# One head further ahead in the gated recurrence: the next head's first direction moved half a head sooner

## The chip, the core and the metric

The kernel runs on one core of one Trainium2 chip. The metric is the device time of one execution in microseconds (us). The engines are TensorE (PE), VectorE (DVE), ScalarE (ACT), GpSimd (POOL) and SyncE (SP, which here issues the DMAs); each works through its own queue in order, and they meet at semaphores.

## The reference, cut to what matters

One layer of a hybrid model: adaLN-modulated RMSNorm, one input projection shared by four retention heads and four heads of a gated linear recurrence (HGRN2), an output projection, then a top-4-of-32 expert FFN. The change touches the recurrence alone. Per head and per direction (forward, backward) over 256 context and 1024 latent tokens:

```
f = lb + (1 - lb) * sigmoid(z)          # z = u @ w_z, per direction
k = 1 - f;  log_a = log(f);  q = silu(u @ w_q);  v = u @ w_v
b = cumsum(log_a) within a chunk
state' = exp(b_end) * state + (k * exp(b_end - b))^T v
out    = causal(q * decay * k) v + (q * exp(b)) state
```

The outputs of both directions are summed, normalised per head and multiplied with a swish gate.

## The kernel before

The stage is `hgrn2`. It holds the projected channels of a head on 128 partitions and the 1280 tokens in the free dimension, in ten tiles of 128 tokens (two context, eight latent). Products of fp32 accuracy are three passes (high, low parts), so one projection of 512 tokens is 24 matmuls. The four heads run one after the other. Head h has two halves: tiles 0 to 3 and tiles 4 to 7.

**PE, for each head h.** Per half `scores` of four tiles and `output` of four, interleaved. Between them stand the projections of the next head: `gates_of_keys(h+1, i)` for i = 0 to 5 (direction d = i // 3; 256, 512 and 512 tokens) and `queries(h+1, 0 and 1)`. After the last `output` come six `turn_keys(h+1, n)` (transposes of the decayed keys), `updates(h+1)` (20 products of turned keys and values) and `gates_of_keys(h+2, 0)` and `(h+2, 1)`. The turned keys go alternately to two PSUM banks, `h_tb` and `h_po`; each has to be copied out by ACT (`turned_keys`) before the bank is written again.

**ACT.** It copies projections out (`copy_z`), splits weights (`high_chunk`), does `logs` (sigmoid of both directions, then log of both), `key_decays` (exp for both directions), `query_sig`, `query_decays`, `totals`, the copies of turned keys, the exps of seven `levels` per half (the first of them as 16 small activations in `first_level`), `roots` (squares of the outputs) and `gate_sig`.

**DVE.** `pick` masks the scores of a tile, `cumulate` scans the logs, `keys`, `decayed_keys` and `decayed_queries` multiply, `level` multiplies the exps of a level with keys and queries, `states` runs the nine-step state chain of a direction, `finish` scales four output tiles, `low_chunk` makes the low parts of the weights.

**POOL.** The subtractions of levels 1 to 6 of each half (four per level), the inverse roots, the gates.

**What sets the order.** Every engine's order is written out by hand, in the loops printed below; there is no planner. The waits that matter for the change:

- `turned_products` waits for the low weights of its chunk (`cw_low`) and, through `group_read`, until the bank used two projections before is read. For `gates_of_keys(h+2, 0)` that reader is DVE's `queries(h+1, 0)`.
- `scores(h, 0)` waits for `states` of direction 0, and for level 6 of that half (`lev_ready`). `scores(h, 3)` and `output(h, 0)` wait for the states of both directions; `output(h, 0)` also for both decayed queries.
- the bank `h_po` holds a half's outputs. `turn_keys` that writes it waits until `finish` has read them.
- `high_early` (ACT, last head only) waits for all `updates`; `low_early` on DVE and `early_rows` on PE, which is work of the next stage done early, wait for it in turn.

Of the kernel before, what the change touches and what calls it, by code (L numbers as in the profile page):

```python
# [366 lines left out]
def hgrn2(nc, m, dram, keep):  # L367
# [3 lines left out]
    with ExitStack() as ctx:  # L371
# [104 lines left out]

        def group(h, i):

            return i if h == 0 else LT + GROUPS * h + i
# [134 lines left out]
        def _(pe):  # L614
# [32 lines left out]
            def gates_of_keys(h, i):  # L647
                d, j = divmod(i, 3)
# [42 lines left out]
            def turn_keys(h, n):  # L691
# [4 lines left out]
                if n == 1:  # L696
                    pe.wait_ge(S["o_ready"], LT * h)
                pe.wait_ge(S["ktok_ready"], 6 * h + max(0, n - 1))
                for i in range(min(4, NT - 4 * g)):
                    c = 4 * g + i  # L700
                    tt = pe.transpose(tb[n % 2][:, i * P:(i + 1) * P], kdec[d][:, c * P:(c + 1) * P], ident[:])
                tt.then_inc(S["turned"], 1)

            def updates(h):
# [4 lines left out]
                for n in range(6):  # L709
                    d, g = divmod(n, 3)  # L710
                    pe.wait_ge(S["ktok_ready"], 6 * h + n + 1)
# [65 lines left out]
            updates(0)  # L777
            for x in range(LT + 2, 2 * LT):
                output_gates(x)
            gates_of_keys(1, 0)  # L780
            gates_of_keys(1, 1)
            for h in range(HEADS):
# [5 lines left out]
                if more:  # L788
                    gates_of_keys(h + 1, 2)
                else:  # L790
# [18 lines left out]
                if more:  # L809
                    for n in range(6):  # L810
# [10 lines left out]
        def _(act):  # L821
# [35 lines left out]
            def copy_z(h, i):  # L857
                d, j = divmod(i, 3)
# [9 lines left out]
            def logs(h):  # L868
                for d in range(2):
                    act.wait_ge(S["z_copied"], 6 * h + 3 * d + 3)  # L870
                    for x, _ in key_pieces(h, d):
                        act.activation(x, x, ACT.Sigmoid).then_inc(S["z_sig"], 1)
# [4 lines left out]
                for d in range(2):  # L877
                    act.wait_ge(S["z_sig"], 4 * h + 2 * d + 2)
                    for (x, _), (to, _), (ahead, _) in zip(key_pieces(h, d), cum_pieces(h), ahead_pieces(h)):
                        act.activation(ahead[:, :, 1:STEP] if d else to, tiles(x) if d else x, ACT.Ln, scale=bound[:, h, d, 1:2], bias=bound[:, h, d, 0:1]).then_inc(S["logf"], 1)  # L880

            def key_decays(h):
                act.wait_ge(S["cumulated"], 6 * h + 3)
# [5 lines left out]
                act.wait_ge(S["cumulated"], 6 * h + 6)  # L889
                act.wait_ge(S["gate_part"], h)  # L890
                for x, part in ahead_pieces(h):
                    act.activation(tiles(kdec[1][:, part]), x[:, :, 0:P], ACT.Exp).then_inc(S["exped"], 1)
# [11 lines left out]
            def totals(h):  # L904
                for x, part in cum_pieces(h):
                    act.activation(total[:, 0, part.start // P:part.stop // P], tiles(x)[:, :, P - 1], ACT.Exp).then_inc(S["totals"], 1)
                for x, part in ahead_pieces(h):
# [10 lines left out]
            def turned_keys(h, n):  # L918
# [4 lines left out]
                act.activation(ktok[d][:, 4 * g:4 * g + m_, :], tb[n % 2][:, 0:m_ * P].rearrange("p (i n) -> p i n", i=m_), ACT.Copy).then_inc(S["ktok_ready"], 1)  # L923
# [79 lines left out]
            logs(0)  # L1003
            value(4)
            value(5)
            key_decays(0)
# [3 lines left out]
            totals(0)  # L1010
# [12 lines left out]
            for x in range(6, 2 * LT):  # L1023
# [3 lines left out]
                if x == LT + 2:  # L1027
                    high_chunk(3)
            gate_sig(0)
# [1826 lines left out]
```

## Time and profile before

| | us |
|---|---|
| three runs | 2736.5, 2736.6, 2742.73 (median 2736.6) |
| profiled execution, span | 2736.2 |
| first scores of head 0, 1, 2, 3 | 209.9, 290.7, 371.6, 464.6 |

The profile was taken on one execution of 2736.2 us, 0.4 us under the median. The recurrence's four heads fill some 300 us of it, from 210 to 507. Times below are counted from the start of the span. "Busy" of PE counts the modelled ends of pipelined matmuls; the starts are exact.

### The profile page before, as it was taken

How to read it: one execution, taken by the hardware profiler on the slowest of the kernel's cores; microseconds unless marked ns; L12 is line 12 of the kernel's file. 1: busy time of each engine (PE TensorE's matmuls, PEld its weight loads, DVE VectorE, ACT ScalarE, POOL GpSimd, SP SyncE). 2: the span in 40 equal slices, each digit the busy share in tenths (PEclk: the TensorE clock that was granted, in tenths of full speed). 3: DMA queues.
4: the chain of work that ended last, by engine and by line, in shares of the span. 5: the costliest groups of instructions: out<-in, count | busy, mean ns of one | idle time of the engine just before them, and what ended most of it. 6: DMA issues, size and time to landing. Idle time of an engine off the chain costs nothing.

```text
span 2736.2 us, 46067 instructions
## 1 busy us (share of the span) xinstructions
PE 2587.9 (95%) x16405; PEld 2212.7 (81%) x16406; DVE 2045.3 (75%) x2500; ACT 1453.7 (53%) x1639; POOL 539.6 (20%) x423
## 2 busy tenths in 40 slices
PE   7998987999896999999999999999999999999995
PEld 3896866777885888777887979899989897898885
DVE  5447888545765987999879787866686778978786
ACT  5446565214443765777557465544454546645554
POOL 0035565200023112121212111110121112111111
PEclk9999998999998999999999999999999999999998
DMA  7121011442333996999879697866586779968783
GB/s 289 39 88 44 22 42 57 173 152 93 109 92 127 386 364 229 365 360 359 287 260 362 235 313 258 283 208 209 190 301 206 247 249 314 344 209 296 261 309 133
DMA packets 274722, 606.26 MB, mean 222 GB/s; under 512 B 21788, under 2 KB 52932, under 8 KB 273520
## 3 DMA queue, kind: packets, MB, share of 16 engines
q1 hardware_dynamic: 254256, 561.62, 57.1%
q0 software_dynamic: 20384, 43.51, 6.9%
q8 instruction: 55, 0.90, 0.1%
q14 instruction: 27, 0.22, 0.0%
HBM read 582.09 MB, written 46.97 MB: 230 GB/s over the span
## 4 chain that ended last, share of the span: by engine, by line
PE 40%; issue 10%; DVE 8%; ACT 4%; DMA 4%; DVEq 1%; POOL 1%; ACTq 0%; POOLq 0%
PE e_acc L2488 7%; PE e_acc L2491 7%; PE e_acc L2489 7%; PE e_acc L2461 5%; PE e_acc L2463 5%; PE e_acc L2462 5%; DMA list_now<-lists 3%; DVE e_slot_r L2646 3%; ACT whi L2574 3%; PE e_tb L2430 1%; DVE yo L2733 1%; DVE e_glu L2709 1%; PE e_acc L2523 1%; DVE e_xlo L2655 1%; POOL sum L2388 1%
## 5 line engine op out<-in xcount | busy, mean ns | idle before, releaser
L2574 ACT ACTIVATE whi<-e_slot 128x2048 fp32r<-128x2048 f32 x296 | 561.0, 1913 | 393.7 <-PE e_acc L2491 327.0
L2646 DVE TENSOR_TENSOR e_slot_r<-e_slot,whi 128x2048 fp32r<-128x2048 f32 x296 | 674.6, 2286 | 106.3 <-ACT whi L2574 106.3
L2488 PE MATMUL e_acc<-e_xhi,whi 128*128 128x256 f32 x1664 | 398.8, 282 | 3.3 <-ACT e_xhi L2578 3.3
L2574 ACT ACTIVATE whi<-slot 128x2048 fp32r<-128x2048 f32 x148 | 283.2, 1913 | 192.4 <-PE e_acc L2463 192.4
L2646 DVE TENSOR_TENSOR slot_r<-slot,whi 128x2048 fp32r<-128x2048 f32 x151 | 344.7, 2285 | 18.1 <-ACT whi L2574 16.5
L2461 PE MATMUL e_acc<-whi,e_ahi 128*128 128x512 f32 x800 | 319.4, 399 | 0.0
L2488 PEld LDWEIGHTS e_acc<-e_xhi,whi 128*128 128x128 f32 x1664 | 313.1, 188 | 6.3 <-ACT e_xhi L2578 6.3
L2463 PE MATMUL e_acc<-whi,e_alo 128*128 128x512 f32 x800 | 313.4, 392 | 0.0
L2462 PE MATMUL e_acc<-e_slot_r,e_ahi 128*128 128x512 f32 x800 | 311.5, 389 | 0.0
L2388 POOL DMA_INDIRECT sum<-yo,e_idx_now x48 | 117.8, 2454 | 973.3 <-issue 518.9
L2461 PE MATMUL e_acc<-whi,e_xhi 128*128 128x512 f32 x768 | 303.6, 395 | 1.8 <-DVE e_slot_r L2646 1.6
L2463 PE MATMUL e_acc<-whi,e_xlo 128*128 128x512 f32 x768 | 302.0, 393 | 0.0
L2334 POOL DMA_INDIRECT e_xg<-v_rows,e_idx_next x74 | 152.3, 2058 | 499.4 <-issue 346.5
L2491 PE MATMUL e_acc<-e_xlo,whi 128*128 128x256 f32 x1664 | 212.7, 282 | 0.0
L2491 PEld LDWEIGHTS e_acc<-e_xlo,whi 128*128 128x128 f32 x1664 | 204.3, 188 | 0.0
L2489 PE MATMUL e_acc<-e_xhi,e_slot_r 128*128 128x256 f32 x832 | 199.2, 281 | 0.0
L2489 PE MATMUL e_acc<-e_xhi,slot_r 128*128 128x256 f32 x832 | 198.0, 280 | 0.0
L2463 PEld LDWEIGHTS e_acc<-whi,e_alo 128*128 128x128 f32 x800 | 149.7, 187 | 34.9
L2462 PEld LDWEIGHTS e_acc<-e_slot_r,e_ahi 128*128 128x128 f32 x800 | 150.4, 188 | 30.9
L2461 PEld LDWEIGHTS e_acc<-whi,e_ahi 128*128 128x128 f32 x800 | 150.5, 188 | 28.6
L2461 PEld LDWEIGHTS e_acc<-whi,e_xhi 128*128 128x128 f32 x768 | 144.6, 188 | 35.3 <-DVE e_slot_r L2646 5.7
L2463 PEld LDWEIGHTS e_acc<-whi,e_xlo 128*128 128x128 f32 x768 | 144.0, 188 | 33.8
(432 smaller groups left out, 5014.9 us busy)
## 6 DMA issues: line engine op xcount, KB each, us to landing
e_slot<-in_w SPq DMA_DIRECT2D x296, 1024.0 KB, 7.1
slot<-in_w SPq DMA_DIRECT2D x151, 1024.0 KB, 6.4
rv<-in_w_ada SPq DMA_DIRECT2D x32, 512.0 KB, 5.6
slot<-in_w_in SPq DMA_DIRECT2D x9, 1024.0 KB, 9.6
wa<-in_w_ada SPq DMA_DIRECT2D x8, 1024.0 KB, 17.1
slot<-in_w_in SPq DMA_DIRECT2D x12, 512.0 KB, 4.2
xt<-in_x SPq DMA_DIRECT2D x8, 512.0 KB, 14.7
slot<-in_w_out SPq DMA_DIRECT2D x4, 1024.0 KB, 13.9
```

What stands on the lines that cost most here:

```text
L2334: g.indirect_dma_start(xg[b][:], None, dram["v_rows"], bass.IndirectOffsetOnAxis(ap=idx_next[:, b:b + 1], axis=0), bounds_check=SEQ - 1, o ...
L2388: g.indirect_dma_start(dram["sum"], bass.IndirectOffsetOnAxis(ap=idx_now[:, b:b + 1], axis=0), yo[:, b, :], None, compute_op=ALU.add).then ...
L2430: tt = pe.transpose(tb[bank][:, k * P:(k + 1) * P], src[:, (4 * at + k) * P:(4 * at + k + 1) * P], ident[:])
L2461: pe.matmul(out, hi[:, k, c], wh, start=False, stop=False)
L2462: pe.matmul(out, hi[:, k, c], wl, start=False, stop=False)
L2463: return pe.matmul(out, lo[:, k, c], wh, start=False, stop=last)
L2488: pe.matmul(out[:, c, :], whi[i % RING][:, w], xhi[:, kk, :], start=first, stop=False, skip_group_check=True)
L2489: mm = pe.matmul(out[:, c, :], wlo[i][:, w], xhi[:, kk, :], start=False, stop=False, skip_group_check=True)
L2491: mm = pe.matmul(out[:, c, :], whi[i % RING][:, w], xlo[:, kk, :], start=False, stop=(kk == KT - 1), skip_group_check=True)
L2523: pe.matmul(out[:, b, :], pick2[:], bias[:, j * 512:(j + 1) * 512], start=True, stop=False)
L2574: act.activation(whi[i % RING][:], raw[i % PIECES][:], ACT.Copy).then_inc(S["whi_made"], 1)
L2646: v.tensor_tensor(wlo[i % PIECES][:], raw[i % PIECES][:], whi[i % RING][:].bitcast(F32), ALU.subtract).then_inc(S["wlo_made"], 1)
```

## The change

Nothing is computed otherwise; instructions move in four queues, and some waits change with them.

- **PE.** All three projections of direction 0 of head h+1 stand before head h begins, the one of 512 tokens of the second half first (`columns`). `turn_keys(h+1, 0..2)` stand in the middle of head h, around `queries(h+1, 0)` and the first score of the second half. Behind the last output comes `gates_of_keys(h+2, 0)`, then turns 3 and 4, updates 0 to 2, turn 5, updates 3 to 5, and two more projections. The turned keys use `h_po` for n = 4 only, all others `h_tb`; so each of turns 1, 2, 3 waits for the copy of the one before. This holds for head 0 too.
- **ACT.** Sigmoid, log and decays are done for direction 0 at the start of head h, for direction 1 behind the levels of its second half. The copy of turn n stands between the levels. `first_level(h+1, 0)` stands before `roots(h, 1)`, `query_decays(h+1)` between level 3 and level 4.
- **DVE.** `cumulate`, `keys`, `decayed_keys` of direction 0 stand between and ahead of the levels of head h's second half. `queries(h+1, 1)` and `finish(h, 1)` stand behind level 1 of the next head, both `decayed_queries` behind level 6, ahead of the second `states`.

```diff
+        def columns(h, i):
+            d, j = divmod(i, 3)
+            return d, (2, 0, 1)[j] if h and d == 0 else j
+        def turn_bank(n):
+            return tb[n == 4]
...
-                if n == 1:
+                if n == 4:
                     pe.wait_ge(S["o_ready"], LT * h)
-                pe.wait_ge(S["ktok_ready"], 6 * h + max(0, n - 1))
+                pe.wait_ge(S["ktok_ready"], 6 * h + (0, 1, 2, 3, 3, 4)[n])
...
-            gates_of_keys(1, 0)
-            gates_of_keys(1, 1)
+            for i in range(3):
+                gates_of_keys(1, i)
...
-                if more:
-                    gates_of_keys(h + 1, 2)
-                else:
+                if not more:
                     early_rows(EARLY_FIRST)
...
                     for i in range(3, 6):
                         gates_of_keys(h + 1, i)
+                    turn_keys(h + 1, 0)
                     queries(h + 1, 0)
+                    turn_keys(h + 1, 1)
...
                     scores(h, j)
+                    if more and j == HT:
+                        turn_keys(h + 1, 2)
...
-                    for n in range(6):
-                        turn_keys(h + 1, n)
-                    updates(h + 1)
                     if h + 2 < HEADS:
                         gates_of_keys(h + 2, 0)
+                    turn_keys(h + 1, 3)
+                    turn_keys(h + 1, 4)
+                    updates(h + 1, range(3))
+                    turn_keys(h + 1, 5)
+                    updates(h + 1, range(3, 6))
+                    if h + 2 < HEADS:
                         gates_of_keys(h + 2, 1)
+                        gates_of_keys(h + 2, 2)
...
@@ scalar @@
-                    for i in range(2):
+                    for i in range(1, 3):
                         copy_z(h + 1, i)
+                    key_sigmoids(h + 1, 0)
+                    key_logs(h + 1, 0)
...
                     levels(h, 1, (l,))
+                    if more and l == 0:
+                        key_decays(h + 1, 0)
+                    if more and l == 1:
+                        copy_z(h + 1, 3)
+                        high_chunk(3 * h + 5)
...
+                    if more and l >= 5:
+                        turned_keys(h + 1, l - 5)
...
+                    key_sigmoids(h + 1, 1)
+                    turned_keys(h + 1, 2)
+                    key_logs(h + 1, 1)
+                    if h + 2 < HEADS:
+                        high_chunk(3 * h + 6)
                     query_sig(h + 1, 0)
+                    key_decays(h + 1, 1)
+                    first_level(h + 1, 0)
...
                     query_sig(h + 1, 1)
+                    turned_keys(h + 1, 3)
+                    levels(h + 1, 0, (1,))
+                    turned_keys(h + 1, 4)
+                    levels(h + 1, 0, (2,))
+                    turned_keys(h + 1, 5)
+                    totals(h + 1, 1)
...
+                    levels(h + 1, 0, (3,))
+                    query_decays(h + 1)
+                    levels(h + 1, 0, range(4, NL))
...
@@ vector @@
                     pick(h, 3)
+                    if more:
+                        cumulate(h + 1, 0)
                     for l in range(NL):
                         level(h, 1, l)
+                        if more and l == 0:
+                            keys(h + 1, 0)
+                        if more and l == 1:
+                            decayed_keys(h + 1, 0)
+                        if l == 2 and more:
+                            low_chunk(3 * h + 5)
...
+                if more and now:
                     keys(h + 1, 1)
                     decayed_keys(h + 1, 1)
+                    if h + 2 < HEADS:
+                        low_chunk(3 * h + 6)
+                    queries(h + 1, 0)
                     for l in range(NL):
                         level(h + 1, 0, l)
+                        if l == 1:
+                            finish(h, 1)
+                            queries(h + 1, 1)
...
+                        if l == NL - 2:
                             states(h + 1, 0)
+                    decayed_queries(h + 1, 0)
+                    decayed_queries(h + 1, 1)
                     states(h + 1, 1)
```

## Rows read from the trace of the kernel before

**Rows 1.** Stretches cut at first scores of halves: span, busy PE, PEld, DVE, ACT, POOL, PEclk, DMA.
```profile
209.88:245.95 36.07, 35.00 (x394) 28.54 (x392) 21.73 (x40) 19.77 (x48) 19.08 (x26) 1.00 0.11 31
245.95:290.74 44.79, 34.76 (x406) 29.07 (x404) 42.81 (x79) 32.51 (x81) 29.33 (x28) 0.85 0.19 51
290.74:326.87 36.13, 34.92 (x393) 28.53 (x393) 24.42 (x49) 20.02 (x49) 19.03 (x26) 1.00 0.11 30
326.87:371.57 44.70, 33.62 (x405) 27.91 (x404) 42.75 (x78) 32.49 (x81) 29.26 (x28) 0.89 0.18 52
371.57:407.72 36.15, 34.95 (x392) 28.53 (x393) 24.38 (x49) 20.01 (x49) 19.04 (x26) 1.00 0.06 16
407.72:464.64 56.92, 39.34 (x406) 32.17 (x405) 48.47 (x87) 34.71 (x81) 30.29 (x28) 0.82 0.21 68
```
**Rows 2.** Timeline of PE, turns of head 2's keys: start, duration, count, idle before with releaser.
```profile
347.80 1.09 PE L701 MATMUL h_po<-ident,h_kdec 128*128 128x128 f32 x4 [4.39 <-issue]
...
354.46 1.09 PE L701 MATMUL h_tb<-ident,h_kdec 128*128 128x128 f32 x4 [3.00 <-ACT h_ktok L923]
```
**Rows 3.** Timeline, head 0's setup: third turn on PE, copy of the second on ACT.
```profile
158.35 0.38 PE L701 MATMUL h_tb<-ident,h_kdec 128*128 128x128 f32 x2
...
160.16 0.59 ACT L923 ACTIVATE h_ktok<-h_po 128x512 f32<-128x512 f32 x1
```
**Rows 4.** Timeline of PE at the end of a projection (24 such matmuls) and the next scores.
```profile
326.64 0.39 PE L644 MATMUL h_pj<-uT_r,slot_r 128*128 128x512 f32 x1
326.87 0.38 PE L728 MATMUL h_ps<-slot,h_wk 128*128 128x128 f32 x2
```
**Rows 5.** Timeline of DVE, levels of head 2's first half, first multiplication of several levels.
```profile
356.55 0.83 DVE L1210 TENSOR_TENSOR h_wk<-h_wk,h_keyA 128x256 f32<-128x256 f32 x1
...
359.08 0.83 DVE L1210 TENSOR_TENSOR h_wk<-h_wk,h_keyA 128x256 f32<-128x256 f32 x1
...
362.87 0.41 DVE L1210 TENSOR_TENSOR h_wk<-h_wk,h_keyA 128x256 f32<-128x256 f32 x1
...
365.42 0.28 DVE L1224 COPY h_state<-h_ps 128x128 f32<-128x128 f32 x1
...
368.80 1.69 DVE L1210 TENSOR_TENSOR h_wk<-h_wk,h_keyA 128x256 f32<-128x256 f32 x1
```
**Rows 6.** Timeline of DVE ahead of those levels: keys, second direction, finish, weights, decayed queries, level 0.
```profile
338.18 0.86 DVE L1174 TENSOR_SCALAR h_keyA<-h_keyA,h_bound 128x768 f32<-128x768 f32 x1
...
342.63 0.98 DVE L1174 TENSOR_SCALAR h_keyA<-h_keyA,h_bound 128x768 f32<-128x768 f32 x1
...
346.59 1.12 DVE L1248 SCALAR_TENSOR_TENSOR slot<-h_po,h_ms,slot 128x128 f32<-128x128 f32 x4
...
348.22 1.60 DVE L1143 TENSOR_TENSOR slot_r<-slot,slot_r 128x1024 fp32r<-128x1024 f32 x1
349.74 3.19 DVE L1197 TENSOR_TENSOR slot<-slot 128x1024 f32<-128x1024 f32 x2
352.85 1.14 DVE L1207 TENSOR_TENSOR h_wk<-h_keyA,h_keyA 128x512 f32<-128x512 f32 x1
```
**Rows 7.** Groups of DVE from 326.87 to 371.57: the largest scan, count, busy, mean ns.
```profile
L1158 DVE TENSOR_TENSOR_SCAN h_cumB<-h_scan,h_cumB 128x512 f32<-128x512 f32 x1 | 1.2, 1202 | 0.0
```
**Rows 8.** Timeline of ACT: the three table loads, then the decayed queries' exps to the totals.
```profile
322.30 1.28 ACT L872 ACT_TABLE_LOAD   x1
...
326.24 1.28 ACT L880 ACT_TABLE_LOAD   x1
...
330.91 1.28 ACT L887 ACT_TABLE_LOAD   x1
...
345.39 0.63 ACT L897 ACTIVATE slot<-h_cumA 128x512 f32<-128x512 f32 x1
...
348.77 0.20 ACT L906 ACTIVATE h_total<-h_cumA 128x6 f32<-128x6 f32 x1
```
**Rows 9.** Timeline of PE ahead of head 3: the first early row, after the last update.
```profile
451.33 0.77 PE L686 MATMUL h_pj<-h_early,uhi 128*128 128x512 f32 x1 [9.34 <-DVE slot_r L1151]
```

More of the change, by code:

```diff
@@ L866, in copy_z, with key_sigmoids, key_logs @@
                 act.activation(to, pj[i % 2][:, 0:z - a], ACT.Copy).then_inc(S["z_copied"], 1)
[L868 to L872, printed above, removed]
+            def key_sigmoids(h, d):
+                act.wait_ge(S["z_copied"], 6 * h + 3 * d + 3)
+                for x, _ in key_pieces(h, d):
+                    act.activation(x, x, ACT.Sigmoid).then_inc(S["z_sig"], 1)
+            def key_logs(h, d):
                 if h:
@@ L876, in logs, with key_decays @@
                     gates_out(act, 2 * LT)
[L877 to L883, printed above, removed]
+                act.wait_ge(S["z_sig"], 4 * h + 2 * d + 2)
+                for (x, _), (to, _), (ahead, _) in zip(key_pieces(h, d), cum_pieces(h), ahead_pieces(h)):
+                    act.activation(ahead[:, :, 1:STEP] if d else to, tiles(x) if d else x, ACT.Ln, scale=bound[:, h, d, 1:2], bias=bound[:, h, d, 0:1]).then_inc(S["logf"], 1)
+            def key_decays(h, d):
+                act.wait_ge(S["cumulated"], 6 * h + 3 * d + 3)
+                if d:
+                    act.wait_ge(S["gate_part"], h)
+                    for x, part in ahead_pieces(h):
+                        act.activation(tiles(kdec[1][:, part]), x[:, :, 0:P], ACT.Exp).then_inc(S["exped"], 1)
+                    return
                 act.wait_ge(S["u_done"], 6 * h)
@@ L888, in key_decays @@
                 k.then_inc(S["exped"], 1)
[L889 to L892, printed above, removed]
             def query_decays(h):
@@ L1009, in _ @@
             value(7)
-            totals(0)
+            for d in range(2):
+                totals(0, d)
             value(8)
@@ L1280, in _ @@
                     pick(h, 3)
+                    if more:
+                        cumulate(h + 1, 0)
                     for l in range(NL):
                         level(h, 1, l)
+                        if more and l == 0:
[4 more added lines that the diff above has]
+                            low_chunk(3 * h + 5)
                         if l == 4:
                             finish(h, 0)
-                        if l == 5 and more:
-                            low_chunk(3 * h + 5)
                     pick(h, HT)
-                if more:
-                    cumulate(h + 1, 0)
+                    pick(h, HT + 1)
+                elif more:
+                    cumulate(0, 0)
+                    keys(0, 0)
                 if h == 0:
@@ L1292, in _ @@
                     set_ahead(aheadB[1])
-                if now:
-                    pick(h, HT + 1)
-                    pick(h, HT + 2)
                 if more:
@@ L1322, in _ @@
                             low_early(1)
-                        if now and l == NL - 2:
+                        if l == NL - 2:
                             states(h + 1, 0)
-                    if not now:
-                        low_chunk(3)
-                        states(0, 0)
+                    decayed_queries(h + 1, 0)
+                    decayed_queries(h + 1, 1)
                     states(h + 1, 1)
+                elif more:
+                    decayed_keys(0, 0)
+                    keys(0, 1)
+                    decayed_keys(0, 1)
+                    low_gates(1)
+                    low_gates(0)
+                    queries(0, 0)
+                    queries(0, 1)
+                    decayed_queries(0, 0)
+                    decayed_queries(0, 1)
+                    for l in range(NL):
+                        level(0, 0, l)
+                    low_chunk(3)
+                    states(0, 0)
+                    states(0, 1)
                 else:
```

75 lines of the change are left out of this document (31 added, 44 removed).

## The prediction

> **What bounds the kernel now.** I read the timelines of the four engines over the recurrence, and cut them at the first scores of each half head. In the first halves, PE is busy 35.0 of 36.1 us while DVE is busy for 22 to 24: PE is the bound. In the second halves DVE is busy 42.8 of 44.7 us and PE only 33.6, part of that at 1.2 GHz (granted clock 0.89 and 0.85 of 2.4 GHz) [rows 1]. So the period of 80.8 us is one half bound by PE and one by DVE. What the change is after is PE's idle time in the DVE half: 4.4 us before the second turn and 3.0 us before the fifth, where it waits for ACT, which stands between them in its own queue [rows 2]. All pauses of such a half add up to 44.7 - 33.6 = 11.1 us, and to 56.9 - 39.3 = 17.6 us before head 3 [rows 1].
>
> I count by two marks per head: T, the first scores of the head, and s, the first scores of its second half. Before, T to s is 36.1 us and s to the next T 44.8, 44.7 and 56.9 us [rows 1]. The change puts one projection of 512 tokens, `gates_of_keys(h+1)`, from behind T to ahead of T. It is 24 matmuls of 0.23 to 0.24 us, 5.7 us [rows 4]. To compare alike I take 5.7 off the first halves (30.4 us) and add it to the two middle second halves (50.5 us); the last, s to T of head 3, has no such projection and stays 56.9.
>
> **Part 1: head 0's setup.** Turns 1, 2 and 3 now share one bank, so turn 2 needs the copy of turn 1. PE reached turn 2 at 158.35, and ACT ended that copy at 160.75, because `first_level` stands before it [rows 3]. PE has no pause around there (busy in each slice from 151 to 202), so it moves back by 2.4 us. Cost: **+2.4**.
>
> **Part 2: the first half, T to s.** PE's own work is 30.4 us less its pauses, plus two turns (0.7 us). But DVE now also has the first direction to do here. Its queue from the fourth pick, which ends at T + 9.1, to level 6: three scans, seven levels, keys, decayed keys, the low weights of one chunk, and `finish`.
> - scans 2.9 us when alone (1.2 us for 512 tokens, 1280 tokens in all [rows 7])
> - level 0 in 3.3 to 3.7, levels 1 and 2 in 2.5 each while POOL works, levels 3 to 6 in 1.3 each without it [rows 5, 6]
> - keys and decayed keys 4.5, weights 1.6, finish 1.1 [rows 6]
>
> The sum is 2.9 + 3.3 + 5.0 + 5.2 + 4.5 + 1.6 + 1.1 = 23.6; with seams 23.9: s = T + 33.0. The queries' projection on PE waits for the same queue: its low weights come behind level 2, at T + 26.7, after PE is ready at T + 25.1; then 5.7 us and a turn give T + 32.8. Both paths end together.
>
 So s = T + 34.2 against 30.4 for head 0: **+3.8**.
>
> For heads 1 and 2 the decayed queries are new between level 6 and the second states: 3.2 us [rows 6]. The first scores start at level 6, but `scores(h, 3)` and `output(h, 0)` need both, so DVE brings first 3.2, then 3.4 us of states (365.42 to 368.80 in [rows 5]), then a pick. The first output starts at T + 7.3 instead of T + 4.2: 3.1 more, and everything behind it. **+6.9** for each.
>
> **Part 3: the middle second halves, s to T.** The gain is meant to come here: DVE has 7.4 us less to do. But its queue is now tied to ACT and PE in turn. The chain, from s on:
> - ACT: copy of turn 1, then sigmoid and log of direction 1. A load is 1.28; both directions with the load take 3.9 and 4.7 us, so one takes 2.6 and 3.0 [rows 8]. With a second copy between: s + 6.7.
> - DVE: scans 3.2 (ten of 128 tokens), two picks 2.0, keys and decayed keys 4.5, low weights 1.6, queries 0.7 [rows 6]: s + 18.8.
> - PE: `gates_of_keys(h+2, 0)` waits for the last two of these. It was ready at s + 15.8. The projection 5.7, turn 3: s + 25.0. This is the new head-of-line wait: ACT stands at the copy of turn 3, with the exps of level 1 behind it, and DVE has nothing from s + 22.5 on.
> - ACT: copy and first exp, s + 26.0. DVE: level 1 and `finish`, s + 29.8. Only then may turn 4 write `h_po`.
> - Turn 4, copy, ten updates, turn 5, copy: s + 33.0. ACT: total, one copy, level 3, then `query_decays`, 3.4 us [rows 8], first exp of level 4: s + 38.8.
> - DVE: levels 4 and 5 2.5, states 3.4, level 6 2.5 because the first multiplication meets POOL's gate (1.69 us) [rows 5]: T = s + 47.2.
>
> PE is ready at s + 43.8, so it waits 3.4 us. Against 50.5 that is **-3.3** for each of two heads. The granted clock is taken as 2.4 GHz here, as pauses are shorter than before; what if not is a rival.
>
> Two table loads more lie on this chain in ACT (sigmoid and log are now loaded twice per head), at 1.28 us each; the row after each load starts 0.01 us behind it. The Trainium skill (ScalarE: Activation LUTs, What ACT_TABLE_LOAD costs) gives a switch 1283 ns and a drain of 1380 ns behind it. By that rule each would cost 2.66 us, and the estimate for three heads would be some 8 us higher; the trace shows no drain, and the sum stands without it.
>
> **Part 4: the last second half.** PE has no projection to do, so turn 3 is at s + 16.9 and level 1 follows at s + 24.0, `finish` s + 25.1, turn 4. By then PE has been idle 8 us; I count updates at 1.2 GHz, as the clock fell in the same place before. Updates end at s + 34.9. Before, PE's last update ended at 442.0 (451.33 less 9.34, [rows 9]), s + 34.3: nothing gained. Then `high_early` 3.7, level 3, and now `query_decays` 3.4 us before level 4, behind which `low_early` stands. So `early_rows(0)` starts at s + 47.4 where it was 451.33 - 407.72 = 43.6: **+3.8**. DVE's levels, states and decayed queries end under the 13 us of early rows.
>
> **Sum.** 2.4 + 3.8 - 3.3 + 6.9 - 3.3 + 6.9 + 3.8 = +17.2 us. Behind head 3's first scores nothing is changed, and the next stage starts at a barrier, so the shift stays. On the span of 2736.2 that is 2753.4; the median lies 0.4 above the profiled span: **2754 us**, 0.6% slower. DMAs are no part: the same loads are issued, and those moved (weights of two chunks, the gates behind `finish`) have over 5 us to spare.
>
> **Rivals.**
> - *It does what it is for, faster.* If ACT and PE never hold up each other, DVE alone bounds a period, with 24.4 + 42.8 + 1.2 = 68.4 us [rows 1] against 80.8. Two periods give up to -24.8; allowing half of it, for picks and gates that have to wait anyway, -12.4, with +2.4 of the setup and no loss elsewhere: -10, 2727 us. For it: DVE's work moved away is real. Against: turn 3 behind a projection, and turn 4 behind `finish`. It decides at whether DVE stands idle after level 0. Chance 0.09.
> - *No difference.* Scans pay nothing to POOL (-3.6), and PE reaches T later than DVE, so that the wait of output 0 is hidden (-6.2): 17.2 - 9.8 = +7.4, 2744 us. Chance 0.17.
> - *Slower still, by the clock.* If TensorE's clock falls to 1.2 GHz in the pause before turn 4, as it did in the pause of 4.4 us before [rows 1, 2], ten updates and a turn take twice 2.4 us, and the chain hangs on them: +2.5 for each of two heads, 2759 us. Chance 0.20.
> - The forecast, 2749 to 2757: chance 0.52. The last 0.02 is beyond.
>
> **Range and chances.** 2740 to 2764 leaves out the faster case and the tails. A difference of under 0.3% (8.2 us) is about what a measurement of this kernel can't tell from none. Faster 0.09; same 0.17; slower 0.74.
>
> **What the profile after would show.** First output of heads 1 and 2 over 7 us behind the first scores, instead of 4.2. DVE idle 3 to 4 us in front of level 1 of each next head, released by ACT. PE idle about 3 us before a projection with DVE as releaser, 4 to 5 us before turn 4. Six table loads per head instead of three. First scores of heads 1, 2, 3 near 299, 384 and 482. The prediction is wrong if PE's pause before T is gone, if level 1 on DVE follows level 0 at once, or if the setup costs nothing.

## The result, and the profile after

| | before | after |
|---|---|---|
| median of four runs | 2738.2 us | 2772.8 us |
| profiled execution, span | 2736.2 | 2775.1 |
| first scores of head 0, 1, 2, 3 | 209.9, 290.7, 371.6, 464.6 | 218.1, 308.9, 401.3, 498.5 |
| start of the next stage | 511.8 | 549.8 |

The ratio is 1.0128, with an interval of 1.0113 to 1.0143: 1.3% slower. In the profiles nearly the whole loss stands at the end of the recurrence: 38.0 us of 38.9. Foretold were 17, and the median of 2772.8 us lies outside the stated range of 2740 to 2764. The profile of after was taken on the slowest of its four executions (2776.8, 2776.5, 2769.2 and 2768.9 us), so the steps below may add up to some 4 us more than the median shows.

The stretches of after, cut at the first scores of halves like [rows 1], which they answer (span, busy PE, PEld, DVE, ACT, POOL, granted clock, DMA share, GB/s; the last is head 3's first half):
```profile
218.09:254.17 36.08, 33.03 (x377) 26.91 (x376) 30.62 (x49) 25.34 (x61) 23.85 (x26) 0.91 0.11 30
254.17:308.91 54.74, 40.91 (x423) 34.38 (x421) 32.37 (x68) 31.44 (x70) 22.37 (x28) 0.85 0.18 51
308.91:346.69 37.78, 33.37 (x377) 27.10 (x378) 35.53 (x60) 25.57 (x62) 23.79 (x26) 0.90 0.06 15
346.69:401.33 54.64, 40.54 (x423) 34.06 (x421) 32.53 (x67) 31.45 (x70) 22.37 (x28) 0.85 0.18 52
401.33:440.03 38.70, 34.64 (x376) 27.87 (x377) 34.92 (x60) 25.48 (x62) 23.17 (x26) 0.87 0.01 1
440.03:498.45 58.42, 37.33 (x396) 31.12 (x397) 38.62 (x68) 33.19 (x69) 23.97 (x28) 0.80 0.21 66
498.45:534.91 36.46, 34.71 (x369) 27.79 (x368) 25.01 (x49) 13.96 (x40) 19.72 (x26) 0.91 0.01 2
```
DVE's work did move as meant: the middle second halves have 32.4 us of it instead of 42.8. But they are not shorter, they are 10 us longer, and no engine is busy in them for more than 41 of 54.7 us. The clock is below 1 in every stretch, while before the first halves ran at 1.00.

PE's timeline from the end of head 0's first half to the first output of head 1 (start, duration, line, operation, count, idle before with its releaser):
```profile
245.38 0.77 PE L651 MATMUL h_pj<-uhi,slot_r 128*128 128x512 f32 x1 [2.96 <-DVE slot_r L1185]
...
272.61 0.79 PE L651 MATMUL h_pj<-uhi,slot_r 128*128 128x512 f32 x1 [2.96 <-DVE slot L1221]
...
281.01 0.60 PE L710 MATMUL h_tb<-ident,h_kdec 128*128 128x128 f32 x4
286.48 1.09 PE L710 MATMUL h_po<-ident,h_kdec 128*128 128x128 f32 x4 [4.88 <-issue]
...
308.91 0.76 PE L737 MATMUL h_ps<-slot,h_wk 128*128 128x128 f32 x2 [6.00 <-DVE h_wq L1257]
315.47 0.46 PE L759 MATMUL h_po<-h_val,h_st 128*128 128x128 f32 x2 [1.40 <-DVE h_near L1286]
```
All the foretold waits are there: 2.96 us before the queries' projection and before `gates_of_keys(2, 0)`, 4.88 before turn 4, and 6.00 before T, where 3.4 were counted. The second projection takes from 272.61 to turn 3 at 281.01, 8.4 us, where 5.7 were counted. Most of it ran at 1.2 GHz: its products start 0.43 us apart until 278.7 and 0.23 us apart after that. That was not in the sum. The first output of head 1 starts at T + 6.56, not over 7 us behind T: the two decayed queries took 2.35 us here, 3.19 in [rows 6].

DVE and POOL: level 1 of head 1, and its level 6 with POOL's gates beside it.
```profile
282.79 0.79 DVE L1252 TENSOR_TENSOR h_wk<-h_wk,h_keyA 128x256 f32<-128x256 f32 x1 [8.36 <-ACT h_wk L990]
...
304.29 1.39 DVE L1252 TENSOR_TENSOR h_wk<-h_wk,h_keyA 128x256 f32<-128x256 f32 x1
305.60 2.56 DVE L1253 TENSOR_TENSOR h_wk<-h_wk,h_keyA 128x256 f32<-128x256 f32 x1
```
```profile
303.05 2.35 POOL L1135 TENSOR_TENSOR slot<-h_kdec,slot 128x1024 f32<-128x1024 f32 x1 [17.23 <-ACT h_kdec L950]
305.48 2.40 POOL L1137 TENSOR_TENSOR slot<-slot,h_nw 128x1024 f32<-128x1024 f32 x1
```
DVE stands idle for 8.36 us between level 0 and level 1, waiting for an exp of ACT, which stands behind the copy of turn 3. Some 2.2 us of that are there because level 0 ended sooner than foretold (s + 20.3, not s + 22.5), the rest is the chain. The second multiplication of level 6 begins 0.12 us behind a POOL product and ends 0.3 us behind that product's end. The Trainium skill (SBUF — State Buffer, Who interferes with whom) calls the port that both need an exclusive lock, so that the later one waits out the other's whole instruction. By that rule, the trace agrees here: 2.56 us for 0.41 us of work.

### The profile page after: what moved, and what is told of

It is laid out like the page before. It is cut to its first block, busy times and chain, and to the rows that moved or that the text cites. A ratio compares the mean times of both kernels' runs of the same rounds, so it can differ in the third digit from the quotient of the medians.

```text
span 2775.1 us, 46091 instructions
## 1 busy us (share of the span) xinstructions
PE 2603.0 (94%) x16405; PEld 2225.2 (80%) x16406; DVE 2048.8 (74%) x2500; ACT 1468.4 (53%) x1648; POOL 535.1 (19%) x423
## 4 chain that ended last, share of the span: by engine, by line
PE 39%; issue 10%; DVE 8%; ACT 4%; DMA 4%; DVEq 1%; POOL 1%; ACTq 0%; POOLq 0%
PE e_acc L2543 7%; PE e_acc L2546 7%; PE e_acc L2544 7%; PE e_acc L2516 5%; PE e_acc L2518 5%; PE e_acc L2517 5%; DMA list_now<-lists 3%; DVE e_slot_r L2701 3%; ACT whi L2629 3%; PE e_tb L2485 1%; DVE yo L2788 1%; DVE e_glu L2764 1%; PE e_acc L2578 1%; DVE e_xlo L2710 1%; POOL sum L2443 1%
## 5 line engine op out<-in xcount | busy, mean ns | idle before, releaser
L2518 PEld LDWEIGHTS e_acc<-whi,e_alo 128*128 128x128 f32 x800 | 149.7, 187 | 34.9
L2516 PEld LDWEIGHTS e_acc<-whi,e_xhi 128*128 128x128 f32 x768 | 144.5, 188 | 35.5 <-DVE e_slot_r L2701 5.8
## 6 DMA issues: line engine op xcount, KB each, us to landing
xt<-in_x SPq DMA_DIRECT2D x8, 512.0 KB, 14.9
```

The source lines that it names most:

```text
L2516: pe.matmul(out, hi[:, k, c], wh, start=False, stop=False)
L2518: return pe.matmul(out, lo[:, k, c], wh, start=False, stop=last)
```

## Experiments

Marks as in the prediction: T is the first scores of a head, s those of its second half. "Idle products" are `pe.matmul(ps[2][:, 384:512], ident, ident)`, before the early rows with `pj[0]` in place of `ps[2]`, into columns that nobody reads at that time; they only keep PE busy. The table has all kernels. A ratio is of medians, against runs of the kernel before on the same chip. Marks and spans are of one profiled execution each, and the executions of one kernel lie up to 9.5 us apart (e9: 2736.3 to 2745.9), so a difference of 1 or 2 us between two rows is not shown to be one.

| kernel | T0 | s to T (1, 2, 3) | T to s (0, 1, 2, 3) | stage ends | span | ratio |
|---|---|---|---|---|---|---|
| before | 209.9 | 44.8, 44.7, 56.9 | 36.1, 36.1, 36.2, 32.2 | 511.8 | 2736.2 | |
| after | 218.1 | 54.7, 54.6, 58.4 | 36.1, 37.8, 38.7, 36.5 | 549.8 | 2775.1 | 1.0128 |
| e1_warm | 218.1 | 55.4, 55.4, 64.5 | 35.5, 39.9, 41.1, 31.7 | 556.3 | 2781.7 | 1.0176 |
| e1b_warm_half | 218.0 | 49.9, 49.1, 54.8 | 34.3, 39.1, 39.0, 37.4 | 536.5 | 2769.3 | 1.0109 |
| e2_queries_early | 217.9 | 50.0, 51.1, 59.8 | 34.7, 37.3, 37.6, 32.2 | 535.6 | 2758.5 | 1.0090 |
| e3_turn_first | 218.6 | 44.3, 43.4, 59.3 | 34.9, 38.6, 40.6, 34.8 | 529.4 | 2750.8 | 1.0067 |
| e4_setup_banks | 215.3 | 54.7, 53.3, 58.5 | 36.1, 39.1, 38.7, 36.5 | 547.0 | 2768.3 | 1.0117 |
| e5_turn_queries | 215.3 | 46.4, 48.1, 58.2 | 34.2, 39.8, 35.6, 32.4 | 524.9 | 2747.3 | 1.0049 |
| e6_and_low_queries | 216.1 | 47.9, 46.9, 57.0 | 34.2, 38.0, 36.8, 32.2 | 524.2 | 2747.1 | 1.0036 |
| e7_low_first | 215.3 | 47.3, 49.0, 57.8 | 34.3, 34.8, 36.9, 32.6 | 523.0 | 2747.0 | 1.0039 |
| e8_gates_wait | 218.7 | 48.2, 50.3, 58.9 | 34.9, 41.3, 41.3, 32.3 | 540.8 | 2764.2 | 1.0098 |
| e9_all | 215.6 | 43.1, 43.3, 50.9 | 34.3, 35.7, 34.9, 31.7 | 504.3 | 2740.2 | 1.0016 |
| e10_before_warm | 209.9 | 44.8, 44.7, 52.3 | 35.9, 38.2, 38.1, 31.7 | 510.5 | 2738.9 | 1.0005 |
| e11_all_cold | 215.6 | 46.1, 44.5, 53.2 | 34.3, 34.8, 35.4, 32.5 | 511.4 | 2737.1 | 1.0006 |
| e12_before_late | 210.2 | 44.8, 44.8, 51.8 | 36.2, 36.1, 36.1, 32.9 | 507.8 | 2728.9 | 0.9982 |

### Is it the clock? Idle products in the pauses

e1_warm puts them before the two projections, before turn 4 and before the early rows; e1b_warm_half has the same with 12, 12, 18 (30 in the last transition) and 44.
```
+                    warm(24)
                     queries(h + 1, 0)
...
+                        warm(24)
                         gates_of_keys(h + 2, 0)
                     turn_keys(h + 1, 3)
+                    warm(40 if h + 2 < HEADS else 60)
                     turn_keys(h + 1, 4)
...
+                        pe.wait_ge(S["q_ready"], 2 * HEADS - 1)
+                        warm(80, pj[0])
```

> The changed kernel with idle products of the identity put ahead of PE's waits: 24 before the queries' projection, 24 before the next head's projection, 40 (60 before head 3) before turn 4, 80 before the early rows; a product takes about 0.12 us, so they fill the pauses of 3.0, 3.0, 4.9 and 7.6 us and little more. Theory (the missing loss is TensorE's clock: projections at 8.5 instead of 5.7 us, updates at 4.5 instead of 2.2): projections back at 5.7 us, 8 to 9 us less for each of heads 0 and 1, some 4 less before head 3, in all 20 to 22 us less than the changed kernel's 2772.8: about 2752, ratio to the kernel before 1.005. Rival (the clock is beside the path, the order alone costs): within 3 us of 2773, although the projections run at 5.7 us.

A miss by its size: one idle product takes 0.22 us on PE, not 0.12. The first 24 took 5.5 us where the pause was 2.96, the 40 before turn 4 took 9.1 where it was 4.88. The clock was up, and both projections took 5.7 us, but the kernel was slower than after, by 11.6 us in the median.

> The idle products of the run before, in about half the number: 12 before the queries' projection, 12 before the next head's, 18 (30 before head 3) before turn 4, 44 before the early rows. One such product took 0.22 us there, not 0.12, so the doubled fill was 5.3 us in a pause of 3.0 and ate what the clock gave back; now it is 2.6 us in 3.0 and 4.0 in 4.9. Theory (the clock is on the path): 20 to 22 us less than the changed kernel's 2772.8, so 2750 to 2753, with projections of 5.7 us. Rival (order alone): 2770 or more, although the projections run at 5.7 us.

The middle second halves, and PE before turn 4 and at T:
```profile
252.26:302.18 49.92, 42.21 (x481) 36.49 (x481) 32.48 (x68) 30.52 (x69) 22.41 (x28) 0.98 0.20 57
302.18:341.29 39.11, 38.42 (x401) 31.56 (x401) 34.99 (x60) 25.42 (x62) 23.15 (x26) 0.81 0.06 15
```
```profile
282.47 0.63 PE L710 MATMUL h_po<-ident,h_kdec 128*128 128x128 f32 x4 [0.94 <-issue]
...
302.18 0.77 PE L741 MATMUL h_ps<-slot,h_wk 128*128 128x128 f32 x2 [6.05 <-DVE h_wq L1266]
```
At a clock of 0.98 the half takes 49.9 us instead of 54.7, the next one 49.1. So the clock costs 5 us in each. The foretold 47.2 plus the 2.0 us by which level 6 was too short in the forecast makes 49.2: the rest of the chain was right. The pause before T stays, since it is DVE's, and the first half behind it falls to 0.81 and gives 1.3 us back. The stage ends 13.3 us sooner than in after, but the whole kernel won only 4.6 in the median, where the theory had 20 to 22 and its rival under 3: neither. Some 7 us were lost again behind the recurrence; the last part of the experiments comes back to them.

### Which order costs what

e2_queries_early: the exps of the decayed queries ahead of the copy of turn 3, the queries and decayed queries between levels 0 and 1.
```
                     query_sig(h + 1, 1)
+                    query_decays(h + 1)
                     turned_keys(h + 1, 3)
...
+                        if l == 0:
+                            queries(h + 1, 1)
+                            decayed_queries(h + 1, 0)
+                            decayed_queries(h + 1, 1)
```

> The changed kernel with the exps of the decayed queries on ACT ahead of the copy of turn 3, and queries(h+1, 1) and both decayed queries on DVE between level 0 and level 1, where DVE stood idle for 8.4 us. Theory (decayed queries behind the levels cost 3.4 us of ACT before level 4 and 3.2 us of DVE before the first output, both on the path): 6.6 us less for each of heads 1 and 2, 3.4 to 5.4 less for head 3: 2754 to 2756. Rival (their place is beside the path, since the path runs over the turns): under 3 us less, 2770 or more.

Middle second halves of 50.0 and 51.1 us, the stage ends 14.3 us sooner. In the median it is 12.2 us, two thirds of what was expected. The work fills a part of the 8.4 us that DVE stood idle before level 1, and is gone from between level 3 and level 4 and from behind level 6. Head 3's first half is back at 32.2.

e3_turn_first: turn 3 ahead of the projection.
```
+                    turn_keys(h + 1, 3)
                     if h + 2 < HEADS:
                         gates_of_keys(h + 2, 0)
-                    turn_keys(h + 1, 3)
```

> The changed kernel with turn 3 ahead of gates_of_keys(h+2, 0) on PE, nothing else. Theory (turn 3 behind a projection that waits for DVE is the head-of-line wait): turn 3 at 271.3 instead of 281.0 in head 0, level 1 on DVE at 275 instead of 282.8, turn 4 then right behind the projection, 4.8 us sooner; for heads 0 and 1, nothing for head 2: 2763. Rival (turn 4 and its updates end the chain by themselves, behind finish and roots): less than 2 us, 2771 or more.

PE at turn 3 and at turn 4:
```profile
270.18 0.66 PE L710 MATMUL h_tb<-ident,h_kdec 128*128 128x128 f32 x4 [1.22 <-DVE h_kdec L1234]
...
277.25 0.39 PE L653 MATMUL h_pj<-uT_r,slot_r 128*128 128x512 f32 x1
278.13 0.63 PE L710 MATMUL h_po<-ident,h_kdec 128*128 128x128 f32 x4 [0.48 <-issue]
```
Turn 3 comes 10.8 us sooner, turn 4 8.4 sooner. The copy, level 1 and `finish` now run beside the projection; from s to turn 4 no pause of 3 or 5 us is left, and turn 4 takes 0.63 instead of 1.09 us. The pause of 6 us before T stays. The middle halves fall to 44.3 and 43.4, the largest single effect: 20.5 us at the stage's end, twice what was expected, since turn 4 came 8.4 us sooner and not 4.8. The wait for a projection and the clock lost behind it came from one step of the order.

e4_setup_banks: in head 0 alone the turns use the two banks in turn again.
```
-            return tb[n == 4]
+            return tb[n == 4 if h else n % 2]
...
-                pe.wait_ge(S["ktok_ready"], 6 * h + (0, 1, 2, 3, 3, 4)[n])
+                pe.wait_ge(S["ktok_ready"], 6 * h + ((0, 1, 2, 3, 3, 4)[n] if h else max(0, n - 1)))
```

> The changed kernel with the two banks taken in turn for head 0's six transposes, as before the change. Theory: the two pauses of 1.1 us at 156 and 161 go, and the end comes 2.3 us sooner: 2770.5. Rival (a later wait takes them up): no difference, 2773.

T0 at 215.3 instead of 218.1: the 2.4 us of Part 1, with 0.4 more.

e5_turn_queries joins e2, e3 and e4. e6_and_low_queries adds to it the weights of the queries (`high_chunk(3 * h + 5)` ahead of the levels on ACT, `low_chunk` behind level 1 on DVE). e7_low_first is e6 with the projection first again, but what it waits for ahead of the keys:
```
+                    if h + 2 < HEADS:
+                        low_chunk(3 * h + 6)
+                    queries(h + 1, 0)
                     keys(h + 1, 1)
                     decayed_keys(h + 1, 1)
```

> Turn 3 ahead of the projection, decayed queries between level 0 and level 1, and head 0's two banks, together. The single gains were 19.8, 12.2 and 4.2 us. If the three waits are links of one chain that add up: 2737 (no difference to the kernel before). If they overlap (the clock was part of both first gains, and DVE's work becomes the bound): 2742 to 2750.

> The same, and the weights of the queries' chunk split before the levels on ACT and right behind level 1 on DVE, ahead of the decayed keys. Theory (PE's wait of 3.0 us before the queries' projection, with the clock falling behind it, is on the path): that wait goes, the first half ends when DVE's levels do, 1.5 to 3 us less for each of three heads than the run with three edits. Rival (DVE's queue, whose sum is the same, ends the first half anyway): under 1 us in all.

> As the last one, but in place of turn 3 ahead of the projection, DVE does the low weights and queries(h+1, 0) before the keys of direction 1, so that PE finds its projection ready. Theory (what matters is that PE never waits there): PE has no pause behind the last output, turn 3 at s + 22 instead of 27, within 4 us of the run before it. Rival (turn 3 early is what matters, since ACT's and DVE's chain hangs on it): 3 us per head slower than that run, 6 to 10 in all.

The gains overlap: e2, e3 and e4 alone give 14.3, 20.5 and 2.9 us at the stage's end, together 24.9. Against e5, e6 ends the stage 0.8 and e7 2.0 us sooner, and the intervals of their three ratios overlap. So e6's rival held: with PE's wait gone, DVE's queue ended the first half. What is filled in one place opens in another: in e6 PE waits 4.5 us before turn 4 and 2.7 before T, in e7 7.4 and 2.7 (head 1), 5.7 and 2.6 (head 2). Three orders ended within 2 us of each other.

### POOL's gates beside level 6

e8_gates_wait is after with one wait in POOL's `gates`.
```
                 g.wait_ge(S["g_sig"], h + 1)
+                g.wait_ge(S["lev_ready"], 2 * h + 1)
```

> The changed kernel, but GpSimd waits for the last level of a head's first half before its two 1024-column products on the gates (4.8 us per head), which in the changed kernel ran beside VectorE's level 6 and stretched two multiplications from 0.41 to 1.39 and 2.56 us. If that contention is part of the loss, level 6 takes 0.41 per multiplication again and each second half gets about 3 us shorter (54.7 to about 51.7), the stage ends 6 to 9 us sooner than in the changed kernel and the span falls by as much. If the products merely slow something else that stands next in VectorE's queue (the states, the picks), the second halves stay within 1 us of 54.7.

DVE at level 6 of head 1 and behind it, and PE's projection before turn 3:
```profile
300.30 0.43 DVE L1253 TENSOR_TENSOR h_wk<-h_wk,h_keyA 128x256 f32<-128x256 f32 x1
300.64 0.42 DVE L1254 TENSOR_TENSOR h_wk<-h_wk,h_keyA 128x256 f32<-128x256 f32 x1
...
301.58 4.53 DVE L1240 TENSOR_TENSOR slot<-slot 128x1024 f32<-128x1024 f32 x2
```
```profile
272.00 0.50 PE L651 MATMUL h_pj<-uhi,slot_r 128*128 128x512 f32 x1 [2.95 <-DVE slot L1222]
...
277.58 0.60 PE L710 MATMUL h_tb<-ident,h_kdec 128*128 128x128 f32 x4
```
Level 6 is back at 0.43 and 0.42 us, 3.1 us less for two multiplications, and the second halves are 6.5 and 4.3 us shorter. Not all of that is the port: this time the projection behind the same pause of 2.95 us took 5.6 us, not 8.4. But the gates now meet the decayed queries (4.53 us for the two, 2.35 in after, 3.2 in [rows 6]), the first half behind runs at a clock of 0.80, and it is 3.5 and 2.6 us longer. From T1 to T3 nothing is won (191.8 us; 189.5 in after); the 9.0 us at the stage's end come from the first head (7.7) and from head 3's first half (4.2).

### Everything, with and without idle products; and the kernel before with one of the moves

e9_all is e7_low_first with the wait of e8, 24 idle products before turn 4 (36 in the last transition), 16 before the early rows, and level 3 ahead of the split of the early weights. e11_all_cold is the same without idle products.
```
                     if h + 2 < HEADS:
                         copy_z(h + 2, 0)
-                    else:
+                    levels(h + 1, 0, (3,))
+                    if h + 2 == HEADS:
                         high_early(0)
                         high_early(1)
-                    levels(h + 1, 0, range(3, NL))
+                    levels(h + 1, 0, range(4, NL))
...
-                        if l == 4 and h + 2 == HEADS:
+                        if l == 3 and h + 2 == HEADS:
                             low_early(0)
```

> The experiment with low parts first (its stage ended at 522.98), and in it: GpSimd's products on the gates behind the last level as in the run beside this one; 24 idle identity products before turn 4 (36 in the last transition), which there waited 7.4 and 10.0 us; 16 more before the projection's early rows; and in the last transition level 3 ahead of the split of the early weights on ScalarE and on VectorE. If the contention of the gates, the half clock behind PE's pauses and the 6.2 us in which VectorE waited for ScalarE's split are all real costs, they are worth about 3 us in each middle second half and 8 to 10 in the last: the stage ends 12 to 16 us sooner, near 508 to 511, at or below the 511.8 of the kernel before. If VectorE's own queue is the limit, as in its first halves (33 us busy of 34 to 37), not more than 5 us come.

> The run before with everything (stage end 504.32, span 2740.2) without its idle products. If the clock is what they bought, turn 4, the updates and the two projections behind them go at half clock again, but VectorE already ends at 292.80 and 457 there: the middle second halves lose 0 to 4 us each and the last one 4 to 6, and the stage ends at 509 to 516. The experts' stage behind it took 203.0 us from its first product to the end of its first tenth, against 197.0 in the kernel before and 197.2 in the kernel with low parts first; the other kernel with idle products there took 203.1 as well. If the idle products cause that, it is 197 here and the span is the stage's end plus 2224 to 2225 us, 2733 to 2741; if the earlier arrival causes it, it stays at 203.

The second and the third stretch and the last transition, of e9 and then of e11:
```profile
249.84:292.95 43.11, 41.85 (x469) 35.89 (x469) 33.47 (x70) 28.33 (x67) 20.62 (x27) 0.96 0.19 54
292.95:328.62 35.67, 30.77 (x376) 24.83 (x377) 33.37 (x58) 28.60 (x66) 28.51 (x28) 1.00 0.11 31
...
406.78:457.72 50.94, 48.09 (x500) 41.56 (x501) 37.66 (x74) 29.72 (x65) 21.02 (x27) 0.90 0.23 76
```
```profile
249.90:295.98 46.08, 40.48 (x421) 34.28 (x421) 32.84 (x70) 28.38 (x67) 20.45 (x27) 0.85 0.18 50
295.98:330.81 34.83, 30.47 (x378) 24.72 (x377) 33.22 (x58) 28.56 (x66) 28.47 (x28) 1.00 0.11 32
...
410.72:463.94 53.22, 38.16 (x397) 31.64 (x397) 39.23 (x78) 30.16 (x66) 23.66 (x28) 0.81 0.23 73
```
e9 ends the stage 7.5 us before the kernel before, and yet its span is 4.0 us longer. Of these 11.5 us, 1.4 are lost ahead of the experts' stage, 6.0 in its first 200 us and 4 behind them. From the stage's first product on, first 20 us at a time, and then the whole stretch; first before, then e9, then e11:
```profile
870.80:890.80 20.00, 16.91 (x91) 15.36 (x92) 12.76 (x15) 5.58 (x6) 5.45 (x3) 0.78 0.41 136
890.80:910.80 20.00, 20.00 (x91) 16.32 (x90) 17.90 (x14) 14.42 (x11) 4.83 (x2) 1.00 1.04 398
870.80:1067.80 197.00, 192.60 (x1068) 165.89 (x1069) 164.12 (x156) 114.25 (x86) 32.41 (x17) 0.98 0.86 310
```
```profile
864.70:884.70 20.00, 11.50 (x75) 10.91 (x76) 12.76 (x15) 4.37 (x5) 5.45 (x3) 0.76 0.38 120
884.70:904.70 20.00, 20.00 (x80) 16.05 (x80) 12.41 (x10) 10.39 (x7) 0.00 (x0) 0.87 1.04 398
864.70:1067.70 203.00, 193.10 (x1068) 166.20 (x1069) 163.96 (x156) 114.22 (x86) 32.32 (x17) 0.96 0.84 301
```
```profile
871.20:1068.30 197.10, 192.29 (x1068) 165.70 (x1069) 163.96 (x156) 114.25 (x86) 32.42 (x17) 0.98 0.86 310
```
The same 1068 products take 203.0 us in e9 and 197.0 and 197.1 in the others. e9's PE is busy 11.5 of the first 20 us and then goes at 0.87. Of the other kernels with idle products, e1b had 202.5 and e10 203.1 here, and e1 195.3. An early arrival is not the reason: e12_before_late comes as early as e9 (864.3) and takes 196.7. So without them e11 keeps what e9 lost, and is level with before: 1.0006, interval 0.9997 to 1.0015, as expected in the upper part of its range.

Nothing that these profiles name as a releaser stands behind the wait, but the DMA queues tell more. Queue 8 is of the kind "instruction" and moves 16 KB at a time; its line in the pages of e11 and of e9:
```profile
q8 instruction: 55, 0.90, 0.1%
```
```profile
q8 instruction: 58, 0.95, 0.1%
```
The eleven kernels without idle products all have 55 such transfers, the four with them 58 (e9), 60 (e10), 61 (e1b) and 62 (e1). PE's longest pause in e9's experts' stage, behind its first product, stands between two products of one group, where the code has no wait:
```profile
884.56 0.58 PE L2527 MATMUL e_acc<-slot_r,e_xhi 128*128 128x512 f32 x1 [5.47 <-issue]
```
A transfer of queue 8 starts at 882.1 in it and ends at 883.1, 1.4 us before PE goes on. The pauses of 4.58 us in e1b (at 955.5) and 4.52 in e10 (at 925.2), 57 us into the stage, hold two such transfers each, and the last one ended 1.8 us before PE went on. e1 and e9 have one more pause, of 3.38 us, 200 and 207 us into the stage; a transfer ends just as it begins. It lies outside the stretch above, so e1 was not spared. So PE seems to wait for its own instructions there: idle products make its instruction stream longer, and the transfers fall at other places. That is an inference from times that fit; no run moves a transfer and nothing else.

e10_before_warm puts idle products into the pauses of the kernel before.
```
                     for n in range(6):
+                        if n in (1, 4):
+                            warm({1: 14, 4: 9}[n])
                         turn_keys(h + 1, n)
...
+                        pe.wait_ge(S["q_ready"], 2 * HEADS - 1)
+                        warm(36, pj[0])
```

> The kernel before, with idle identity products in the pauses of its turns (14 before turn 1, 9 before turn 4) and 36 before the projection's early rows. VectorE ends its middle second halves there (42.8 us busy of 44.8), so a full clock on TensorE is worth nothing in them: second halves of 44 to 45 as before. In the last transition the early rows ran at half clock (13.5 us for 48 products, right ahead of the first scores): at full clock they take 5.8 and the last second half falls from 56.9 by 5 to 7 us. If the clock was a cost in the kernel before too, the middle halves shorten by 2 to 3 us each as well.

The middle halves stay at 44.8 and 44.7: bound by DVE, as the prediction's first part read them. But the first halves behind them grow from 36.1 to 38.2 and 38.1, at a granted clock of 0.91 where they had 1.00: what was kept up in one half fell in the next. The last second half falls by 4.6, 5 to 7 were expected. The reason given there was half wrong: the 48 products are two early rows, not one, and take 11.1 us at full clock, so 2.3 us come from them and 2.3 from the updates before.

e12_before_late is the kernel before with level 3 ahead of the split, the diff of e9 above.

> The kernel before, with one thing: in the last transition level 3 ahead of the split of the early weights on ScalarE and VectorE. VectorE idled 5.35 us there for level 3, and the early rows waited 9.34 us for the split's low part, which ended at 453.39. It should end at 450.5 or so, and the early rows (13.5 us at half clock) and the first scores behind them follow: last second half 54 instead of 56.9, stage and span 3 us less, 2733 to 2734. If PE's clock or another wait takes it back, no change. It tells how much of what the run with everything gained in its last transition was to be had without the change.

PE's first early row, which answers [rows 9]:
```profile
446.35 0.76 PE L686 MATMUL h_pj<-h_early,uhi 128*128 128x512 f32 x1 [4.48 <-DVE slot_r L1152]
```
It waits 4.48 us instead of 9.34. The last transition takes 51.8 us (54 were expected), less than the 53.2 of e11, and the kernel is the fastest of all: 0.9982, interval 0.9973 to 0.9991, 4.5 us. So what e9 and e11 win in their last transition doesn't need the change.

## Why the prediction was wrong in size

The direction was right, and so was the order of the waits, but +17 was foretold where the profiled span grew by 38.9 and the median by 34.6. The direction rested on Parts 1, 2 and 4; Part 3, which had a gain of 3.3 us for each of two heads, came out as a loss of 4.2 (54.7 against 50.5). By the stage's end, 38.0, step by step:

| step | foretold | measured | miss |
|---|---|---|---|
| Part 1, setup (T0, less 5.7 for the projection) | +2.4 | +2.5 | +0.1 |
| Part 2, first half of head 0 | 34.2 | 36.1 | +1.9 |
| Part 2, first halves of heads 1, 2 | 37.3 | 37.8, 38.7 | +1.9 |
| Part 3, middle second halves | 47.2 | 54.7, 54.6 | +14.9 |
| Part 4, last second half | 60.7 | 58.4 | -2.3 |
| head 3's own first half | 32.2 | 36.5 | +4.3 |

- **Part 1: right.** e4 undid it.
- **Part 2: right for DVE, wrong for PE.** Level 6 ended at T + 34.1, and the scans beside POOL paid somewhat less than assumed: 3.7 us for the three, where 2.9 alone and 4.1 with POOL were counted. The row that answers [rows 7]:
```profile
228.64 1.58 DVE L1200 TENSOR_TENSOR_SCAN h_cumB<-h_scan,h_cumB 128x512 f32<-128x512 f32 x1
```
  1.58 instead of 1.20 us. "Both paths end together" failed in head 0: the queries' projection took 8.5 us, not the 5.7 of the sum, since the clock had fallen in the pause of 2.96 us before it. In heads 1 and 2 the same projection took 7.2 and 5.7 us behind pauses of 2.93 and 2.59 us; there the first scores ran at 1.2 GHz as well, behind the pause of 6 us before T.
- **Part 3: the step that failed.** "The granted clock is taken as 2.4 GHz here, as pauses are shorter than before" was a choice, with a rival beside it, and it was wrong: the clock fell to 1.2 GHz for most of `gates_of_keys(2, 0)` and again for turn 4 and its updates. Of the 7.5 us, the projection is 2.7, turn 4 to the start of turn 5's copy 2.6 (5.8 us, where 3.2 were counted), and level 6 beside the gates 2.0 (4.5 where 2.5 were counted: the row it was sized from met the gates with one multiplication, here two met them). e1b took the first two away, e8 the third.
- **Part 4: nearly right**, 2.3 us too much: the updates ended at s + 32.5, not s + 34.9. PE's pause before the early rows was 12.5 us.
- **The end of the sum: wrong.** "Behind head 3's first scores nothing is changed" forgot that `output(3, 0)` waits for the decayed queries as those of heads 1 and 2 do. I had put the 3.1 us on two heads of three, and the clock came on top (0.91, [rows 1] has 1.00 for first halves). e2 put them early, and this half was back at 32.2.
- **The rivals.** "Slower still, by the clock" had the right mechanism, but priced only the updates: 2.5 per head. The clock also took both projections and the first scores. "Faster" hung on DVE not standing idle after level 0. It did, for 8.36 us, twice what was foretold. "No difference" hung on scans that pay nothing and on PE reaching T behind DVE: the scans paid, and PE waited 6.00 us for DVE at T.
- **The table loads: right.** Six per head, and no drain behind them; ACT in after:
```profile
254.99 1.28 ACT L886 ACT_TABLE_LOAD   x1
256.28 0.84 ACT L886 ACTIVATE h_keyA<-h_keyA 128x768 f32<-128x768 f32 x1
```

Is the idea wrong, or its order? Compared alike, with the moved projection in the second halves, before has 30.4 and 50.5. e11, the best order tried, has 34.3 to 35.4 and 44.5 to 46.1. The second halves win 4.4 to 6.0 us, and the first halves pay 3.9 to 5.0 for it, since DVE is busy 33.2 of head 1's 34.8 us and its levels there run beside POOL. The idea moves work from one bound half into the other; with the waits repaired that comes to nothing, and with the waits as they were it cost 34.6 us. Whether an order exists that wins is not shown.

## What to carry to other kernels

When an instruction that the chain hangs on stands behind a long block on its engine, ask what that block waits for: here one transpose behind one projection cost 20 us over two transitions, and moving it was one line. When a change leaves TensorE with pauses of some 3 us or more, price what follows them at the lower clock, all of it, and take the cheaper case only as the rival. And check the neighbouring work with the kernel before: the one version found that beats it is a level put ahead of a weight split, which has nothing to do with the change.

## What the runs showed of the hardware

- **The clock can halve in a pause of 3 us, but need not.** The projection behind the pause of 2.96 us took 8.4 us in after, the same one behind 2.95 us took 5.6 in e8. A pause of 5.59 us in e11 was followed by turn 4 at 1.09 us, one of 0.48 in e3 by the same turn at 0.63.
- **Large POOL products stretch small DVE multiplications:** each ended 0.3 us behind the product that it met, so 0.41 us became 1.39 and 2.56 beside products of 2.35 and 2.40 us; in e8, apart from them, 0.43 and 0.42.
- **Idle products were not free later.** In three of four kernels with them, PE lost 5.5 to 6.1 us in the first 200 us of a stage 400 us and more behind; in the fourth it had a pause of 3.38 us just after these. The three long pauses hold 16 KB transfers of the instruction queue, and the four kernels have 58 to 62 such transfers, all others 55. The same kernel without them (e11) lost nothing there.
